# Prompt attention in half steps: scores issued pair by pair, between two halves of products and transposes

## The reference, cut to what matters

```
s = einsum('bqghd,bgqkd->bghqk', q_rot, k_sel) * SCALE          # selected branch
p_slc = softmax(where(smask, s, NEG_INF)); o_slc = p_slc @ v_sel
s = einsum('bqghd,bwgd->bghqw', q_rot, wk) * SCALE              # window branch
p_win = softmax(where(wmask, s, NEG_INF)); o_win = p_win @ wv
o = gates[..., 0:1] * o_cmp + gates[..., 1:2] * o_slc + gates[..., 2:3] * o_win
```

## Time and profile before

| | us |
|---|---|
| median of 3 runs | 1474.06 (1468.99 to 1474.79) |
| profiled execution, its own time | 1474.22 |
| its span | 1472.3 |
| TensorE busy in the span | 1415.4 (96%) |
| VectorE, ScalarE, GpSimd busy | 539.8, 454.5, 588.4 |

### The profile page before, as it was taken

One profiled execution on the slowest core, in us unless ns is written; L12 is line 12 of the kernel. 1 busy time (PEld: TensorE's weight loads), 2 busy tenths in 40 slices (PEclk: granted clock), 3 DMA queues, 4 the chain that ended last, 5 costly groups with the idle time before them and its releaser, 6 DMA issues.

```text
span 1472.3 us, 26844 instructions
## 1 busy us (share of the span) xinstructions
PE 1415.4 (96%) x10914; PEld 1306.2 (89%) x10914; DVE 539.8 (37%) x769; ACT 454.5 (31%) x687; POOL 588.4 (40%) x262
## 2 busy tenths in 40 slices
PE   6997999999999999999989999998999999999998
PEld 6997999999999999999857545557999999999997
DVE  5349343222223343215345555542342222223342
ACT  5411243222222333212202555541332222222332
POOL 6332343334434565433300444440333444335562
PEclk8998999999999999999998999999999999999999
DMA  5212122332232323353441000015233222322322
GB/s 194 86 59 86 60 86 87 104 95 85 85 87 78 94 83 116 99 146 101 140 92 52 12 1 1 1 44 165 61 91 108 85 85 85 102 80 79 91 85 78
DMA packets 208062, 124.03 MB, mean 84 GB/s; under 512 B 30964, under 2 KB 205100, under 8 KB 207998
## 3 DMA queue, kind: packets, MB, share of 16 engines
q1 hardware_dynamic: 207998, 123.14, 28.5%
HBM read 117.75 MB, written 5.38 MB: 84 GB/s over the span
## 4 chain that ended last, share of the span: by engine, by line
PE 43%; issue 39%; POOL 14%; SPq 2%; DVE 1%; DMA 1%; ACT 0%; POOLq 0%; DVEq 0%; ACTq 0%
PE PG L431 32%; POOL WL L1646 10%; PE M L1022 3%; PE M L1035 3%; PE PG L987 2%; POOL PB L871 2%; POOL SQX L1641 1%; PE PG L991 1%; SPq L792 1%; SPq L791 1%; PE M L1029 1%; PE M L1136 0%; POOL WBD L838 0%; SPq L787 0%; PE M L915 0%
## 5 line engine op out<-in xcount | busy, mean ns | idle before, releaser
L1646 POOL TENSOR_TENSOR WL<-WR,WH 128x2048 fp32r<-128x2048 f32 x105 | 484.8, 4618 | 668.9 <-ACT WH L491 668.9
L431 PE MATMUL PG<-H,WH 128*128 128x260 f32 x4128 | 672.0, 285 | 17.5 <-DVE P L1869 11.0
L431 PEld LDWEIGHTS PG<-H,WH 128*128 128x128 f32 x4128 | 569.0, 190 | 20.4 <-DVE P L1869 11.4
L431 PE MATMUL PG<-H,WL 128*128 128x260 f32 x2064 | 417.8, 284 | 0.0
L431 PEld LDWEIGHTS PG<-H,WL 128*128 128x128 f32 x2064 | 319.8, 189 | 0.0
L431 PE MATMUL PG<-G,WH 128*128 128x260 f32 x1920 | 308.7, 283 | 1.5 <-DVE G L1407 1.5
L491 ACT ACTIVATE WH<-WR 128x2048 fp32r<-128x2048 f32 x105 | 200.4, 1908 | 277.3 <-PE PG L431 245.1
L431 PEld LDWEIGHTS PG<-G,WH 128*128 128x128 f32 x1920 | 263.2, 189 | 1.6 <-issue 1.6
L431 PE MATMUL PG<-G,WL 128*128 128x260 f32 x960 | 193.8, 283 | 0.0
L431 PEld LDWEIGHTS PG<-G,WL 128*128 128x128 f32 x960 | 148.3, 189 | 0.0
L871 POOL TENSOR_SCALAR PB<-PB,ST,GT 128x128 f32<-128x128 f32 (+3 forms) x128 | 76.4, 611 | 162.9 <-DVE ST L1278 162.2
(11 more groups left out here) (234 smaller groups left out, 995.1 us busy)
## 6 DMA issues: line engine op xcount, KB each, us to landing
WR<-in_w_ffn_in SPq DMA_DIRECT2D x88, 512.0 KB, 4.6
WR<-in_w_in SPq DMA_DIRECT2D x32, 512.0 KB, 4.4
WR<-in_w_ffn_out SPq DMA_DIRECT2D x32, 384.0 KB, 3.6
WR<-in_w_ffn_out SPq DMA_DIRECT2D x32, 320.0 KB, 3.1
WR<-in_w_in SPq DMA_DIRECT2D x18, 256.0 KB, 3.5
WR<-in_w_out SPq DMA_DIRECT2D x8, 512.0 KB, 3.9
PST<-in_cache_kv SPq DMA_DIRECT2D x32, 128.0 KB, 2.1
WR<-in_w_out SPq DMA_DIRECT2D x16, 256.0 KB, 5.8
```

The lines of the kernel that those rows point to most:

```text
L431: mm = pe.matmul(PG[:, par, hf, 0:HALF], w, x, start=(first and at_k == 0 and n == 0), stop=(last and at_k == nk - 1 and n == 2))
L1646: w_split.on(pool.tensor_tensor(WL[:, b, :], WR[:, b, :], WH[:, b, :].bitcast(F32), ALU.subtract))
```

## The change: what it does

TensorE's step becomes two half steps. In each stand a half of the value products of step hu - 1, a half of the transposes of step hu, and the scores of one pair of step hu + 2. `part` cuts a list of banks in two, the smaller half first; with one bank the first half is empty. The two score products of a pair now share one wait, for both exponentials of the pair. VectorE's half step is: reciprocal of step hu + 1, drains, maximum of step hu + 2. ScalarE's is: exponentials of step hu + 1, drains. Block results, the clears and the sample work keep their place.

```diff
-            def scores(hu):
+            def scores(hu, jj):
...
-                for x, (jj, e) in enumerate(HEADS):
-                    if hu:
-                        pe.wait_ge(exp_done.sem, 4 * (hu - 1) + x + 1)
+                if hu:
+                    pe.wait_ge(exp_done.sem, 4 * (hu - 1) + 2 * jj + 2)
+                for e in range(2):
...
-            compress(1, {16: lambda: scores(0)})
+            compress(1, {16: lambda: scores(0, 0), 18: lambda: scores(0, 1)})
...
-                for n in range(0, max(len(now), len(late)), 2):
-                    for q, kt in now[n:n + 2]:
+                for jj in range(2):
+                    for q, kt in part(late, jj):
+                        pv(hu - 1, q, kt)
+                    for q, kt in part(now, jj):
                         turn(hu, q, kt)
-                    for q, kt in late[n:n + 2]:
-                        pv(hu - 1, q, kt)
-                if hu + 2 < len(STEPS):
-                    scores(hu + 2)
+                    if hu + 2 < len(STEPS):
+                        scores(hu + 2, jj)
...
+            for jj in range(2):
+                row_max(1, jj)
             for hu in range(len(STEPS)):
...
                 for jj in range(2):
                     if hu + 1 < len(STEPS):
-                        row_max(hu + 1, jj)
-                    for q, rows in bs[2 * jj:2 * jj + 2] if jj == 0 else bs[2:]:
+                        norm(hu + 1, jj)
+                    for q, rows in part(turned(hu), jj):
                         drain_pt(dve, 0, q, rows)
-                if hu + 1 < len(STEPS):
-                    for jj in range(2):
-                        norm(hu + 1, jj)
-                    if 4 <= hu < 8:
-                        pad_queries(hu - 4)
+                    if hu + 2 < len(STEPS):
+                        row_max(hu + 2, jj)
+                if 4 <= hu < 8:
+                    pad_queries(hu - 4)
...
+        def part(x, jj):
+
+            return x[len(x) // 2:] if jj else x[0:len(x) // 2]
...
                 for jj in range(2):
-                    for q, rows in bs[0:2] if jj == 0 else bs[2:]:
-                        drain_pt(act, 1, q, rows)
                     if hu + 1 < len(STEPS):
                         exps(hu + 1, jj)
+                    for q, rows in part(turned(hu), jj):
+                        drain_pt(act, 1, q, rows)
```

More of the change, by code:

```diff
@@ L974, in cmp_scores @@
                 cs_done.on(mm)
-            def scores(hu):
+            def scores(hu, jj):
                 gp, i, jp, br = STEPS[hu]
                 n = (i + 1) * P
-                if hu == 0:
+                if hu == 0 and jj == 0:
                     pe.wait_ge(cs_out.sem, 2)
@@ L988, in scores @@
                               start=True, stop=False)
-                    if e:
-                        for ee in range(2):
-                            s_done.on(pe.matmul(PG[:, jj, ee, n - P:n], CBF[:, 0:P], CBF[:, P:2 * P], start=False, stop=True))
+                for e in range(2):
+                    s_done.on(pe.matmul(PG[:, jj, e, n - P:n], CBF[:, 0:P], CBF[:, P:2 * P], start=False, stop=True))
             for m in range(KD):
@@ L1050, in pe_attention @@
             q_fill.on(mm)
-            scores(1)
+            for jj in range(2):
+                scores(1, jj)
             for hu in range(len(STEPS) + 1):
@@ L1308, in dve_attention @@
                     o_low(hu // 4 - 1)
-                bs = turned(hu)
                 for jj in range(2):
                     if hu + 1 < len(STEPS):
-                        row_max(hu + 1, jj)
-                    for q, rows in bs[2 * jj:2 * jj + 2] if jj == 0 else bs[2:]:
+                        norm(hu + 1, jj)
+                    for q, rows in part(turned(hu), jj):
                         drain_pt(dve, 0, q, rows)
-                if hu + 1 < len(STEPS):
-                    for jj in range(2):
-                        norm(hu + 1, jj)
-                    if 4 <= hu < 8:
-                        pad_queries(hu - 4)
+                    if hu + 2 < len(STEPS):
+                        row_max(hu + 2, jj)
+                if 4 <= hu < 8:
+                    pad_queries(hu - 4)
             o_low(len(PAIRS) - 1)
```

## The result

| us | before | after |
|---|---|---|
| median | 1471.53 (1466.59 to 1474.79), 4 runs | 1453.87 (1452.90 to 1457.83), 4 runs |
| profiled execution, its own time | 1474.22 | 1453.67 |
| its span | 1472.3 | 1451.6 |

The ratio is 0.9887, 95% interval 0.9861 to 0.9914: 1.1% faster. Both belong to the result, and how far two measurements of one kernel lie apart is half of the lesson.

The account below looks back on a forecast made before the run. Late GpSimd scalings, behind VectorE's reciprocals and drains, were taken to hold up TensorE in prompt attention. Block gains of 13.7 us less 1.7 for waits gave 12: 1474.2 - 12 = 1462.2, forecast 1462, range 1456 to 1471.

Parts of the forecast that it names:

- what bound the kernel: Prompt attention: VectorE's reciprocals behind a drain make GpSimd's four scalings (3.03 us) late for TensorE; some 23 us not work.
- the sum over the blocks: Attention stage: the gains and losses forecast block by block add up to 13.7 us gained.
- The wait of 0.9 forecast for block 0's scores behind a drain: Block 0, first half: TensorE's scores wait 0.9 us for exponentials behind ScalarE's drain, otherwise 0.3.
- In the last block the wait of 0.9: Last step: transposes wanted 5.0 us after the last scores, scalings end at 5.9; 0.9 wait instead of about 3.
- the two waits for a third bank: Five-bank step, block 3: the third transpose waits for a drain to free PSUM, about 0.5 us, twice.
- rival A: Every product behind a mask pays 0.15 us, 8.4 in all; time 1470.5; chance 0.19 together with the key-load rival.
- Rival B: ScalarE's drains ahead of exponentials hold up TensorE's scores, 0.9 us in each of 32 steps; 1489; chance 0.07.
- Each of the 32 mid-step score groups now waits on a semaphore of its own: TensorE's mid-step scores: extra semaphore waits at 0.05 us each, 1.7 taken off the 13.7 us gain.
- Profiled execution: 1474.2 us outside: Starting point of the sum: one profiled execution at 1474.2 us, from which 12 is subtracted.
- The windows outside 808 to 986 unchanged: Sign of the forecast: the profile's windows outside the attention stage stay as they were.
- Rival D: Better than thought: first block at full clock, GpSimd never late; gain 17, 1457 us; chance 0.74 together with the forecast.
- Rival C: Sample stage's key loads hide the gain, time 1474; chance 0.19 together with the mask-cost rival.

Follow-up runs that it names:

- e2: Kernel before, with only the first pair's reciprocal moved ahead of the second half's drains on VectorE: 1465.39 us, ratio 0.9955.
- e1: Changed kernel, with both reciprocals of a step again behind VectorE's last drain: 1491.41 us, ratio 1.0134.
- e9: Changed kernel, with drains again ahead of the exponentials in ScalarE's half step: 1555.98 us, ratio 1.0577.
- e8: Changed kernel, with each score product again waiting for its own head's exponential: 1456.33 us, ratio 0.9901.
- e3: Changed kernel measured once more without any edit: 1458.06 us, ratio 0.9914.
- e5: Changed kernel, with lists of one or two banks left uncut, all in the first half: 1458.83 us, ratio 0.99.
- e6: Changed kernel, with ScalarE's weight copy moved from the end of step 1 to the end of step 31: 1452.28 us, ratio 0.9875.
- e7: Changed kernel, with lists of up to two banks whole in the first half and the weight copy at step 31's end: 1452.54 us, ratio 0.9895.

## Why the forecast was right in kind and short in size

**Right: what bound the kernel.** VectorE's reciprocals stood behind a drain, so that GpSimd's scalings were exposed. e2 takes half of the gain by moving one of them, e1 loses the gain and more by moving both back.

**Right: the sum over the blocks,** 13.7 against 13.9. Its errors are small and cancel, which is luck: two executions of the changed kernel give 13.9 and 12.8, so they differ by more than this forecast misses. The first block is 0.5 too short, blocks 1 and 3 by 0.3 and 0.2, the second block 0 is 0.9 and the last 0.6 too long. The wait of 0.9 forecast for block 0's scores behind a drain is shorter in the timeline of TensorE:

```profile
892.05 0.70 PE L987 MATMUL PG<-KP,QR 64*128 64x256 f32 x4 [0.74 <-ACT PB L1468]
...
895.25 0.70 PE L987 MATMUL PG<-KP,QR 64*128 64x256 f32 x4 [0.26 <-ACT PB L1468]
```

In the last block the wait of 0.9 did not come at all, and the two waits for a third bank were 0.35 each instead of 0.5.

**Right: nothing is paid behind a mask,** rival A. The choice of 0 from a range of 0 to 8.4 was made from the nearest rows, against the rule of the Trainium skill that a change of tiling mode drains the engine (TensorEngine Tiling (Array Packing), Key Properties). The chain above has the products at 852.24 right behind the mask at 852.02, in their usual 0.58. The page gives no price; at the 0.15 of the other changes of kind, 56 places would make the stage 8.4 us longer, and the blocks show no room for it. So the trace doesn't agree with the rule at these places.

**Right: the order on ScalarE decides.** Rival B did not come, because the exponentials stand ahead of the drains; e9 shows what happens where they don't: 95 us of stage, and not the 29 that B priced. B's price was a single wait per step, but the loop closes in each half step and the clock falls with it.

**Wrong, first step: "Each of the 32 mid-step score groups now waits on a semaphore of its own; at 0.05 each I take off 1.7".** It was a term without a row, and the edit doesn't give it either: before, each of a step's four score products waited for its own exponential, now each pair waits once, so the scores have half as many waits as before. Scores at 853.41 stand in the chain directly behind transposes that end there, and e8, with 62 waits more, has the same stage. As far as e8 can tell the term is 0, the stage gains 13.9, and the forecast was 1.9 short by this and the small errors together.

**Wrong, second step: "Profiled execution: 1474.2 us outside" and "the median of the runs shown is 1474.06, the same within 0.2", with "The windows outside 808 to 986 unchanged".** The sum starts at one execution and at a median of three. That execution had the spell at half clock ahead of the stage; the profiled execution of the changed kernel did not, and started the stage 7.4 us earlier, so the windows outside were not unchanged. Over more runs the kernel before has a median of 1471.5 (4), 1471.3 (17) and 1471.2 (11), some 3 below where I started.

This second step is what put the measured time outside the range. Moved down by the 2.7 that the start was too high, the range would begin at 1453.3 and hold 1453.9; moved down by the 1.9 of the first step alone, it would begin at 1454.1 and not hold it. The miss of 8.3 us, from 1462.2 to 1453.9, has three parts: 2.7 is the start (1474.2 against 1471.5), 1.9 the stage's gain (13.9 against 12), and 3.7 is left over, by which the four runs of the changed kernel beat 1471.5 - 13.9 = 1457.6. e3's 1458.1 has no such rest. Does the clock explain it? Here the shortest and the longest run of each, time and mean clock of the whole execution:

```
before   1465.97 at 0.985     1477.35 at 0.977
changed  1452.90 at 0.984     1457.83 at 0.981
e3       1454.76 at 0.985     1461.12 at 0.981
```

Shorter runs tend to have the higher mean clock. A straight line through all 28 runs of before gives 0.8 us for 0.001 of clock, and one through the ten of the changed kernel (first measurement and e3) 1.0. The four runs have a mean clock of 0.984, those of e3 0.983, so clock accounts for about 1 of the 3.7 us. The rest stays open: four runs that lie at the fast end would do it, and so would another chip, since the chip of the first measurement is not on record. The intervals of the two measurements overlap (0.9861 to 0.9914, 0.9891 to 0.9936). Nor was it settled what starts the spell.

**Missed in the range:** it held the unknown costs of the change, but had nothing for the spread of the executions that both kernels were compared by. Rival D, 1457, was nearest to the time; its scalings that are never late came, its first block at full clock did not (0.90, and 0.80 in e3). Rival C did not come: the sample stage's keys are asked for behind the last product in both kernels, and the stage's gain reached the end.

## What to carry to other kernels

Where an engine works in order, ask of each small instruction whose result another engine waits for (here a reciprocal of 0.16 us) what stands ahead of it, and for whom that waits: moving it ahead of a drain was worth 6.9 us of 178 by itself, and standing two exponentials behind a drain cost 95. Move the producers on all engines together, since the new order on TensorE and ScalarE with late reciprocals on VectorE was slower than before. Before a forecast of 1% is summed from one execution, compare its clock by windows with other executions where the change touches nothing, and leave out any term for which no row speaks.

## What the runs showed of the hardware

The same TensorE order ran in 768 to 785 at PEclk 1.00 in some executions and at 0.51 to 0.60 in others (e1, e5, e8, e9 against the changed kernel and e3). The stage began 5.1 to 8.8 us later in those (7.4 in the kernel before), some 0.5% of this kernel. One profile for each of two kernels can show such a difference and seem to speak of the change.

A pair of bf16 mask products over the whole array is followed by fp32 products 64 columns wide 0.22 us after its start, just as by transposes or scores. Between fp32 transposes and those products the 0.15 us remains, in both kernels (one bank 0.58, two 1.01, three 1.45).

A wait of 2.5 us on TensorE (809.34 in the changed kernel) was followed by 5 us at 0.69 of the clock, in e3 at 0.50. In e8 the wait was 2.2, and 815 to 820 ran at 0.66. Without the copy that caused it (e6) the stretch ran at 1.00, and in e5, which has the copy but no wait over 0.75 us in this block, all of the first block did. In e7 the stretch ran at 0.57 with no wait over 0.74 either, so a long wait is not the only way to it.
